# Three rounded products in place of fp32 for the experts' down products, their weights split by ScalarE, VectorE and GpSimd

## The reference

```python
top_i, top_w = route(h2, w_router, router_bias)          # 8 of 64 experts for each token
...
def block(args):                                         # up to 128 rows of one expert
    tok, e = args
    return swiglu(h_pad[tok], w_gate[e], w_up[e], w_down[e])
...
out = out.reshape(n_rows, D) * row_w[:, None]
return jax.ops.segment_sum(out, row_tok, num_segments=T + 1)[:T]
```

## Time and profile before

| | |
|---|---|
| median of 3 runs | 2043.4 us (2042.04 to 2045.72) |
| profiled execution, its own time | 2049.2 us |
| its span, first to last instruction | 2047.6 us |
| mean granted TensorE clock | 0.975 of full speed |
| blocks (scatter-adds) in the expert stage | 92 |
| expert stage in the span | about 1,060 to 2,005 us |

### The profile page before, as it was taken

One profiled execution on the slowest core, in us unless ns is written; L12 is line 12 of the kernel. 1 busy time (PEld: TensorE's weight loads), 2 busy tenths in 40 slices (PEclk: granted clock), 3 DMA queues, 4 the chain that ended last, 5 costly groups with the idle time before them and its releaser, 6 DMA issues. The chain is left out here.

```text
span 2047.6 us, 34503 instructions
## 1 busy us (share of the span) xinstructions
PE 1928.1 (94%) x10264; PEld 1495.0 (73%) x10265; DVE 1038.1 (51%) x1532; ACT 874.1 (43%) x1210; POOL 373.5 (18%) x337
## 2 busy tenths in 40 slices
PE   4999999899899999989789999999999999999995
PEld 3999999899788666755547777777777777777772
DVE  4113401166438335545426666666666666666665
ACT  5110111244212212221246666666666666666663
POOL 0100100111111000000212222232223222222220
PEclk9999999899899999999889999999999999999997
DMA  7211311111443665425069896999998888897964
GB/s 260 74 52 41 123 52 31 32 63 62 144 142 113 229 230 206 143 85 196 1 228 347 261 346 182 317 295 300 331 301 271 269 273 306 244 352 253 300 180 172
DMA packets 182101, 399.64 MB, mean 195 GB/s; under 512 B 22425, under 2 KB 87185, under 8 KB 182046
## 3 DMA queue, kind: packets, MB, share of 16 engines
q1 hardware_dynamic: 149166, 312.16, 42.5%
q0 software_dynamic: 31680, 82.49, 15.7%
q10 hardware_dynamic: 1200, 4.26, 0.6%
HBM read 351.27 MB, written 80.64 MB: 211 GB/s over the span
## 5 line engine op out<-in xcount | busy, mean ns | idle before, releaser
L2184 DVE TENSOR_TENSOR wexp_lo<-wexp,wexp_hi 128x2048 fp32r<-128x2048 f32 x190 | 426.9, 2288 | 91.3 <-ACT wexp_hi L2135 88.3
L2135 ACT ACTIVATE wexp_hi<-wexp 128x2048 fp32r x190 | 353.4, 1907 | 52.4 <-issue 49.4
L2111 PE MATMUL bank<-wexp_down,hTe 128*128 x736 | 330.6, 592 | 0.0
L2086 PE MATMUL bank<-wexp_hi,x_hi 128*128 128x512 f32 x744 | 300.5, 404 | 3.8 <-DVE wexp_lo L2184 3.8
L2086 PE MATMUL bank<-wexp_hi,x_lo 128*128 128x512 f32 x744 | 292.0, 393 | 0.0
L2086 PE MATMUL bank<-wexp_lo,x_hi 128*128 128x512 f32 x744 | 290.4, 390 | 0.0
L2059 POOL DMA_INDIRECT acc_d<-ob,ixs x92 | 153.7, 1670 | 615.8 <-DMA acc_d<-ob,ixs 441.9
L2111 PEld LDWEIGHTS bank<-wexp_down,hTe 128*128 128x128 f32 x736 | 139.1, 189 | 139.4 <-issue 132.3
L547 PE MATMUL bank<-hT_hi,w_hi 128*128 128x344 f32 x576 | 187.3, 325 | 7.3 <-DVEq L659 7.3
L547 PE MATMUL bank<-hT_hi,w_lo 128*128 128x344 f32 x576 | 185.1, 321 | 0.0
L547 PE MATMUL bank<-hT_lo,w_hi 128*128 128x344 f32 x576 | 184.6, 320 | 0.0
(11 more groups left out here) (357 smaller groups left out, 2988.7 us busy)
## 6 DMA issues: line engine op xcount, KB each, us to landing
wexp<-in_w_exp_gate SPq DMA_DIRECT2D x128, 512.0 KB
wexp<-in_w_exp_up SPq DMA_DIRECT2D x128, 512.0 KB
wexp_down<-in_w_exp_down SPq DMA_DIRECT2D x128, 512.0 KB
wada<-in_w_ada SPq DMA_DIRECT2D x12, 2048.0 KB, 10.9
w_raw<-in_w_in SPq DMA_DIRECT2D x44, 512.0 KB, 3.9
gates_d<-gst POOLq DMA_DIRECT2D x48, 172.0 KB, 2.1
gate<-gates_d SPq DMA_DIRECT2D x16, 516.0 KB, 5.8
xn<-in_x_prompt ACTq DMA_DIRECT2D x8, 512.0 KB, 8.3
```

The costliest lines, as they stand in the source:

```text
L2086: last = pe.matmul(banks[0][:].rearrange("p (g n) -> p g n", g=2), stat[:, b, k, :], mov[:, b, :, k * FF:(k + 1) * FF], start=(k == 0 and ...
L2111: last = pe.matmul(banks[4 + half][:], hT[:, f, :], wdn[:, bass.ds(slot, 1), f, half * 512:half * 512 + 512].rearrange("p a n -> p (a n)") ...
L2135: act.activation(w_hi[:, b, g, :], wexp[:, bass.ds(e & (RING - 1), 1), g, :].rearrange("p a n -> p (a n)"), ACT.Copy).then_inc(whi_ok, 1)
L2184: dve.tensor_tensor(w_lo[:, b, g, :], wexp[:, bass.ds(e & (RING - 1), 1), g, :].rearrange("p a n -> p (a n)"), w_hi[:, b, g, :], ALU.subtr ...
```

## The change

The down products become three rounded products as well. The hidden rows, when turned, are rounded by ScalarE (`hTe_hi`) and their remainder is formed by VectorE (`hTe_lo`). The down weights are split into `down_hi` and `down_lo`, each with one buffer (not a ring), in two halves of 512 columns: of the first half ScalarE does the rounding (between its two roundings of gate/up weights) and VectorE the remainder; of the second half GpSimd does both. A half is split for block i+1 once the down products of block i have read it. SP's ring of down weights has 2 slots instead of 4, freed when both remainders are done. GpSimd splits first, then scatters block i, then gathers block i+6. VectorE does the first gate/up remainder of block i+3, the down remainder of block i+1, then in the next block the hidden rows' remainder and the second gate/up remainder. `hh` shares the buffer of `sg`. Each half of the down products signals `dn_ps` by itself.

```diff
-            wdn = far("wexp_down", [P, RING, FF // P, D])
+            wdn = far("wexp_down", [P, 2, FF // P, D])
...
-        hh = tile("hh", [P, FF])
-        hT = tile("hTe", [P, FF // P, P])
+        hh = sg
+        hT_hi = tile("hTe_hi", [P, FF // P, P], F32R)
+        hT_lo = tile("hTe_lo", [P, FF // P, P], F32R)
+        d_hi = tile("down_hi", [P, 2, FF // P, 512], F32R)
+        d_lo = tile("down_lo", [P, 2, FF // P, 512], F32R)
...
+        def down_half(e, half):
+
+            return wdn[:, bass.ds(e & 1, 1), :, 512 * half:512 * half + 512].rearrange("p a f n -> p (a f) n")
...
# SP
                 def next_down(part, g):
-                    at, slot = part * EG + g, g % RING
-                    before = blocks_to(at - 3)
+                    at = part * EG + g
+                    before = blocks_to(at - 1)
                     sp.wait_ge(down_in, 32 * at)
-                    sp.wait_ge(dn_ps, before)
-                    load_down(sp, a, wdn, expert_at(part, g), slot, down_in)
+                    sp.wait_ge(dlo0_ok, before)
+                    sp.wait_ge(dlo1_ok, before)
+                    load_down(sp, a, wdn, expert_at(part, g), g % 2, down_in)
...
# GpSimd
+                def split_down(e, j):
+                    pool.wait_ge(down_in, e * 32 + 32)
+                    if j is not 0:
+                        pool.wait_ge(dn_ps, 2 * j)
+                    pool.sem_inc(passed, 1)
+                    pool.tensor_copy(d_hi[:, 1], down_half(e, 1)).then_inc(dhi1_ok, 1)
+                    pool.wait_ge(dhi1_ok, j + 1)
+                    pool.sem_inc(passed, 1)
+                    pool.tensor_tensor(d_lo[:, 1], down_half(e, 1), d_hi[:, 1], ALU.subtract).then_inc(dlo1_ok, 1)
...
                 def block_of(i, q):
                     b = q % 2
-                    pool.wait_ge(x_tp, i + 3)
-                    pool.wait_ge(wc_ok, i + 3)
-                    gather(i + AHEAD, (q + AHEAD) % RING)
+                    split_down(entry(pool, i + 1, 1, E - 1), i + 1)
                     pool.wait_ge(ob_ok, 2 * i + 4)
...
+                    pool.wait_ge(x_tp, i + 3)
+                    pool.wait_ge(wc_ok, i + 3)
+                    gather(i + AHEAD, (q + AHEAD) % RING)
...
# TensorE, block_of
-                    pe.wait_ge(hT_ok, i + 1)
+                    pe.wait_ge(hTlo_ok, i + 1)
                     pe.wait_ge(ob_ok, 2 * i + 2)
-                    pe.wait_ge(down_in, e * 32 + 32)
                     for half in range(2):
+                        pe.wait_ge(dlo1_ok if half else dlo0_ok, i + 1)
                         for f in range(FF // P):
-                            last = pe.matmul(banks[4 + half][:], hT[:, f, :],
-                                             wdn[:, bass.ds(slot, 1), f, half * 512:half * 512 + 512].rearrange("p a n -> p (a n)"),
-                                             start=(f == 0), stop=(f == FF // P - 1))
-                    last.then_inc(dn_ps, 1)
+                            for n, (stat, mov) in enumerate(((hT_hi, d_hi), (hT_hi, d_lo), (hT_lo, d_hi))):
+                                last = pe.matmul(banks[4 + half][:], stat[:, f, :], mov[:, half, f, :],
+                                                 start=(f == 0 and n == 0), stop=(f == FF // P - 1 and n == 2))
+                        last.then_inc(dn_ps, 1)
...
# ScalarE
+                def round_down(e, j):
+                    act.wait_ge(down_in, e * 32 + 32)
+                    if j is not 0:
+                        act.wait_ge(dn_ps, 2 * j - 1)
+                    act.sem_inc(passed, 1)
+                    act.activation(d_hi[:, 0], down_half(e, 0), ACT.Copy).then_inc(dhi0_ok, 1)
...
-                    act.activation(hT[:].rearrange("p f n -> p (f n)"), banks[3][:, 0:FF], ACT.Copy).then_inc(hT_ok, 1)
+                    act.activation(hT_hi[:].rearrange("p f n -> p (f n)"), banks[3][:, 0:FF], ACT.Copy).then_inc(hThi_ok, 1)
                     take(i + 2, b)
                     gate(i + 1)
-                    round_weights(i + 3, 1 - b)
-                    act.wait_ge(dn_ps, i + 1)
+                    round_weights(i + 3, 1 - b, lambda: round_down(entry(act, i + 1, 1, E - 1), i + 1))
...
# VectorE
+                def rest_of_down(e, j):
+                    dve.wait_ge(dhi0_ok, j + 1)
+                    dve.tensor_tensor(d_lo[:, 0], down_half(e, 0), d_hi[:, 0], ALU.subtract).then_inc(dlo0_ok, 1)
+
+                def turned(j):
+                    dve.wait_ge(hThi_ok, j + 1)
+                    dve.tensor_tensor(hT_lo[:].rearrange("p f n -> p (f n)"), banks[3][:, 0:FF],
+                                      hT_hi[:].rearrange("p f n -> p (f n)"), ALU.subtract).then_inc(hTlo_ok, 1)
...
                 def block_of(i, q):
                     b = q % 2
+                    turned(i)
+                    rest_of_weights(entry(dve, i + 2, 1, E - 1), i + 2, b, 1)
                     take(i + 2, b)
                     to_gather(i + AHEAD, (q + AHEAD) % RING)
                     gate(i + 1)
...
-                    rest_of_weights(e, i + 3, 1 - b)
+                    rest_of_weights(e, i + 3, 1 - b, 0)
+                    rest_of_down(entry(dve, i + 1, 1, E - 1), i + 1)
```

More of the change, by code:

```diff
@@ L1917, in experts @@
         ixs = [tile(f"ixs{b}", [P, 1], U32) for b in range(2)]
-        names = "ix ixs tp xhi xlo wc whi wlo gu sg h hp hT dn ob scat wu wd pad".split()
-        (ix_ok, ixs_ok, x_tp, xhi_ok, xlo_ok, wc_ok, whi_ok, wlo_ok, gu_ps, sg_ok, h_ok, h_tp, hT_ok, dn_ps, ob_ok, added,
-         up_ok, _, pad_ok) = (sem("s6" + n) for n in names)
+        names = "ix ixs tp xhi xlo wc whi wlo gu sg h hp hThi hTlo dhi0 dhi1 dlo0 dlo1 dn ob scat wu pad".split()
+        (ix_ok, ixs_ok, x_tp, xhi_ok, xlo_ok, wc_ok, whi_ok, wlo_ok, gu_ps, sg_ok, h_ok, h_tp, hThi_ok, hTlo_ok, dhi0_ok, dhi1_ok,
+         dlo0_ok, dlo1_ok, dn_ps, ob_ok, added, up_ok, pad_ok) = (sem("s6" + n) for n in names)
         passed = sem("s6passed")
@@ L1988, in _ @@
                         landed_up(j - 1 - RING, 1)
-                next_down(0, RING)
+                        next_down(0, j - 3)
                 with sp.Fori(1, GRP) as part:
@@ L2013, in _ @@
                 n = blocks_done(sp)
-                sp.wait_ge(wlo_ok, n * 2 + 6)
+                sp.wait_ge(wlo_ok, n * 2 + 5)
                 sp.sem_inc(ended, 1)
@@ L2017, in _ @@
                 sp.sem_inc(ended, 1)
-                sp.wait_ge(dn_ps, n)
+                sp.wait_ge(dn_ps, 2 * n)
+                sp.wait_ge(dlo0_ok, n + 1)
+                sp.wait_ge(dlo1_ok, n + 1)
                 sp.sem_inc(ended, 1)
@@ L2104, in block_of @@
                     up(i + 1, 1 - b)
[L2105 to L2106 removed]
+                    pe.wait_ge(hTlo_ok, i + 1)
                     pe.wait_ge(ob_ok, 2 * i + 2)
[L2108 removed]
                     for half in range(2):
+                        pe.wait_ge(dlo1_ok if half else dlo0_ok, i + 1)
                         for f in range(FF // P):
[L2111 to L2114 removed]
+                            for n, (stat, mov) in enumerate(((hT_hi, d_hi), (hT_hi, d_lo), (hT_lo, d_hi))):
+                                last = pe.matmul(banks[4 + half][:], stat[:, f, :], mov[:, half, f, :],
+                                                 start=(f == 0 and n == 0), stop=(f == FF // P - 1 and n == 2))
+                        last.then_inc(dn_ps, 1)
                 blocks(pe, block_of)
                 n = blocks_done(pe)
[L2118 removed]
+                pe.wait_ge(wlo_ok, n * 2 + 5)
                 pe.wait_ge(ob_ok, n * 2 + 2)
@@ L2129, in take, with round_weights @@
                                        banks[1 + half][:], ACT.Copy).then_inc(xhi_ok, 1)
-                def round_weights(j, b):
+                def round_weights(j, b, amid=None):
                     e = entry(act, j, 1, E - 1)
@@ L2134, in round_weights @@
                     for g in range(2):
+                        if g and amid:
+                            amid()
                         act.activation(w_hi[:, b, g, :],
@@ L2148, in _ @@
                 round_weights(2, 0)
+                round_down(entry(act, 0, 1, E - 1), 0)
                 def block_of(i, q):
@@ L2160, in block_of @@
                     for half in range(2):
+                        act.wait_ge(dn_ps, 2 * i + half + 1)
                         act.activation(ob[:, b, 512 * half:512 * half + 512], banks[4 + half][:], ACT.Copy,
@@ L2179, in weight, with rest_of_weights @@
                     dve.tensor_copy(wcol[:, q:q + 1], xg[:, q, bass.ds(e + D, 1)]).then_inc(wc_ok, 1)
[L2181 to L2186, removed]
+                def rest_of_weights(e, j, b, g):
+                    dve.wait_ge(whi_ok, 2 * j + g + 1)
+                    dve.tensor_tensor(w_lo[:, b, g, :],
+                                      wexp[:, bass.ds(e & (RING - 1), 1), g, :].rearrange("p a n -> p (a n)"),
+                                      w_hi[:, b, g, :], ALU.subtract).then_inc(wlo_ok, 1)
```

(13 more changed lines are left out.)

4 lines of the change are left out of this document (1 added, 3 removed).

## The result

The changed kernel takes 2114.3 us (median of 4 runs, 2110.8 to 2117.8) against 2043.1 us (4 runs, 2042.0 to 2045.7): ratio 1.0346, 95% interval 1.0326 to 1.0366. It is slower by 71 us, where 28 were forecast. The span of the profiled execution is 2111.9 us.

The account below looks back on a forecast made before the run. TensorE was taken to bound the expert stage at 10.02 us a block; VectorE and GpSimd excluding each other would make it 10.3, +26 us over 92 blocks, +2 for the first: 2043.4 + 28 = 2071 us, range 1990 to 2115.

Parts of the forecast that it names:

- TensorE's gain: Expert stage, down products: twelve rounded products take 2.74 us for 3.43; period 9.33 us, 63 us saved over 92 blocks.
- Exclusion by whole instructions: Expert stage: VectorE's two-SBUF-input subtractions and GpSimd's SBUF reads wait for each other's end; 9.03 us exclusive work per block.
- port term: Expert stage: VectorE and GpSimd taking turns at SBUF make a block 10.3 us, +0.28 us in each of 92.
- the second: Order two, expert block: VectorE's first subtraction gets in before GpSimd's, so VectorE is the bound at 10.1 us.
- VectorE's own work: Expert block: VectorE's present 6.39 us plus down remainder 1.23 and hidden rows' remainder 0.34, 7.96 us in sum.
- order one: Expert block: GpSimd's subtraction comes ahead of VectorE's first weight subtraction; 21.0 us for two blocks, 10.5 each.
- the likeliest case: Expert stage: the forecast itself, 10.1 to 10.55 us a block, 2052 to 2090 us; chance 50%.
- The scatter chain: Rival, expert stage: if the port costs little, mean landing of 9.5 to 9.9 us floors the period; 1996 to 2032 us; 18%.
- the forecast's terms: GpSimd's work per expert block: cast 1.04 us and subtraction 2.35, beside 2.85 us of indirect DMA issues.
- The exposed register loads: Expert stage, VectorE: taken as nothing; as a rival 0.7 us a block, 2110 to 2135 us; chance 15%.
- Down weights late: Rival, expert stage: two-slot ring delivers down weights late; with a lower clock 2080 to 2150 us, together 5%.
- The clock: Expert stage: pauses of about 1 us a block don't lower TensorE's clock; rival shared with late down weights, 2080 to 2150, 5%.

Follow-up runs that it names:

- e6: Changed kernel with down weights split for block 0 alone and each scatter-add moving 256 of 1024 columns: 1984.8 us.
- e3: Changed kernel with each scatter-add moving 256 of 1024 columns, the rest of the expert result left out: 2088.8 us.
- e4: Changed kernel with GpSimd's cast and subtraction replaced by three fills of the same tiles, which read nothing: 2048.6 us.
- e5: Changed kernel with down weights split for block 0 alone, later blocks using that split; rounded products, hidden rows' split and waits stay: 2020.6 us.
- e1: Changed kernel with GpSimd splitting nothing: ScalarE rounds and VectorE subtracts both halves of the down weights: 2063.1 us, ratio 1.0074.
- e7: Changed kernel with ScalarE and VectorE doing the whole split and each scatter-add moving 256 of 1024 columns: 2044.9 us.
- e2: Changed kernel with the register load for VectorE's second gate/up subtraction issued before the hidden rows' subtraction: 2116.8 us.
- e10: Changed kernel without GpSimd's splitting (ScalarE and VectorE do it), register load hoisted, four buffers for the scatter's index column: 2050.1 us, ratio 1.0012.
- e11: Changed kernel, GpSimd still splitting, with the register load hoisted and four buffers for the scatter's index column: 2105.9 us, ratio 1.0297.

## Why the prediction missed by 43 us

**TensorE's gain: right.** Twelve rounded products at 0.227 us, 2.73 us for the 2.74 forecast; 9.27 us a block in `e6` for 9.33, 60 us for 63.

**Exclusion by whole instructions: right**, shown by the timelines of after and `e3`, and by `e4`, where GpSimd reads nothing and neither engine's instructions grow.

**The size of the port term: nearly right.** Forecast 10.3 us a block, measured 10.45 with the landing relieved (`e3`), which is 38 to 46 us over the kernel before, by the median on its own chip or on the first. The order that came about is the second, put at 10.1: it was short by a cast that costs 0.64 and not 0.15, and by the 0.34 taken off for the hidden-row subtraction, which stands beside nothing; VectorE's own work came out 0.39 lower than summed, 7.57 for 7.96, and hid part of that. The price of order one hit the number by chance. (The upper end of the likeliest case, 10.55 us, comes by the forecast's own sum to 2094 us, not 2090; nothing hangs on it.)

**The scatter chain: here the prediction failed.** It made the landing a rival, "if the port costs little", a floor of 9.5 to 9.9 us that a port at 10.3 would cover. The floor's height was right (9.77 in `e5`). But it isn't covered: a shorter scatter-add takes 25 us off the kernel after (`e3`) and 18 off `e1` (`e7`), where a floor below the engines' own period should have given nothing.

The landings themselves tell why, taken over 1,300 to 1,900 us from the start of a scatter-add to the last event of its landing. In the kernel before they take 8.93 us in the mean, and 51 of 59 next scatter-adds start within 1.0 us of one: that chain, 9.8 us a step, lay only 0.2 us under TensorE's 10.02, though TensorE never paused. In the kernel after they take 9.40 us, and 38 of 54 start so. And a landing varies, 5.1 to 13.2 us in these 54. Read so, a long landing sets one block and the port the next, and the mean lies above what either gives alone: 10.83 us, or 10.64 without the blocks in which the clock was low, against 10.3 by the mean landing (9.40 and 0.9 until the next) and 10.46 in `e3`.

And GpSimd takes its queue in order: wait for the landing, scatter, gather, then the next split, of which TensorE needs the result. By the code a late landing moves the cast and the subtraction, and these then hold VectorE at another place; that last link is argued, not shown by a run. In the block shown GpSimd waited 2.51 us for a landing. What was left out is also that GpSimd's queue leaves little room: 8.73 us of 10.83, where the forecast's terms make 6.25, since its two indirect DMAs grew from 2.85 us a block to 4.29 (2.25 + 2.04) and its subtraction from 2.35 to 3.41.

**The sum, cut another way**, by four kernels of which each puts back one thing: 2045.2 before; 1984.8 with rounded products alone (`e6`, -60); 2020.6 with the whole scatter-add (`e5`, +36); 2048.6 with the first half split and GpSimd occupied (`e4`, +28); 2114.3 with GpSimd's reads (+66). The chips differ by up to some 7 us, so each step is good to about that (against the kernel before on each chip they are -60, +36, +23 and +73). In the other order the landing is worth 25 (`e3` to after, the clock's part included) or 18 (`e1` less `e7`): it overlaps with the rest in part, but never wholly.

**The exposed register loads: rightly taken as nothing in the sum** in this kernel (`e2`); whether it pays by itself where the port is free wasn't tried, since `e10` has two edits at once.

**Down weights late: small.** ScalarE waits 4.8 us in the 600 for their landing.

**The clock: the prediction had it wrong too.** It took from the earlier trace rows that pauses of about 1 us a block don't lower it, and put a lower clock among its smallest rivals. In the kernel after it fell six times in the window, for 23.9 us, at half rate; there is no other such stretch from 1,060 to 2,060 us, so the loss is at most 12 us. The 9 blocks that such a stretch touches take 11.77 us in the mean, from transposes to transposes, the other 46 take 10.64; `e3`, with none, takes 10.46. By this the 0.53 us a block that were missed (10.83 for 10.3) are 0.15 of the port, some 0.2 of the landing and some 0.2 of blocks with a lower clock. The last share is an upper bound: a long block may be why the clock falls. Whole executions point the same way: the four of `e11` took 2098.4, 2101.5, 2110.4 and 2119.6 us at a mean granted clock of 0.975, 0.975, 0.971 and 0.969. Which is cause and which effect no run shows.

**Open:** whether a gather issued ahead of the scatter would take part of the 25 us away, why the landing takes 5 us in one block and 13 in another, and how much of the 25 us the clock has. None of these was tried.

## What to carry to other kernels

A change that relieves the bounding engine is worth what the next limit leaves: here 60 us by TensorE, of which a chain of transfers takes 36 before any new work is paid for. Don't treat two limits of nearly one height as alternatives when one in-order queue joins them; add a part of the second, and look at how much its single steps vary. Before such a change, see how far the next limit lies below the first: here a chain of landings lay 0.2 us a block under TensorE, which was busy without a pause. And don't split subtractions of two SBUF tensors between VectorE and GpSimd as here: giving all of it to VectorE and ScalarE cost 51 us less, with more work on both.

## What the runs showed of the hardware

GpSimd's issue of an indirect DMA is held by VectorE's subtractions too. In the kernel after, the gather that starts at 1511.03, right behind the start of VectorE's subtraction (1510.90 to 1513.17), takes 3.08 us. In the kernel before it takes 1.05 us at 1504.67, ahead of VectorE's pair of subtractions (from 1505.25), and 2.78 at 1515.70, inside the next pair (from 1515.27). Over 1300 to 1900 us of the kernel before, the 52 gathers that don't start inside a weight subtraction take 1.05 us in the mean, the 8 that do take 2.26, and each of the 8 ends 0.9 us after that subtraction. In the kernel after 48 of 56 start inside one, and their mean is 2.38 us. A scatter-add is held in the same way, and ends 1.5 us after the subtraction. The other way round nothing is seen: in `e1`, with the gathers at 2.14 us, VectorE's weight subtractions keep 2291 ns. The Trainium skill ("SBUF — State Buffer", "Who interferes with whom") names this for VectorE's copies, and has a subtraction of two tensors not do it, with a reason that it calls inferred; these rows say that here it does. Whether it is the reading of the indices or the writing of the transfers that is held, no run tells apart.

A fill on GpSimd of 128x1024 takes 955 to 969 ns in the mean beside VectorE's work (`e4`), a subtraction of the same size 2352 alone and 4153 in `e3`.
